# First attention of a two-block kernel: scores in plain fp32, and probabilities turned in 32x32 pieces on VectorE and moved inside SBUF

## The chip, the cores and the metric

The kernel runs on one core of one Trainium2 chip. The metric is device time in microseconds (us), the median of several runs. Engines: PE is TensorE (PEld its weight loads), DVE VectorE, ACT ScalarE, POOL GpSimd, SP SyncE. A suffix q (SPq, POOLq) is an engine's own sequencer, which issues DMAs. SBUF is the on-chip memory of 128 partitions, PSUM the banks that PE writes.

## The reference

Two layers on one sequence of 512 tokens and 1024 channels. The first has a convolution mixer and a dilated attention of 8 heads of 64 channels, and a gated feed-forward; the second has a state-space mixer and a sparse attention. The change touches the first attention:

```python
q = rms_norm(q.reshape(B, S, N_HEADS, HEAD_DIM), g_q[l]) * (HEAD_DIM ** -0.5)
k = rms_norm(k.reshape(B, S, N_HEADS, HEAD_DIM), g_k[l])
y_attn = dilated_mixture(q, k, v).reshape(B, S, D_ATTN)
# dilated_mixture: for (window, dil) in ((128, 1), (512, 4), (2048, 16)) a causal, strided
# softmax attention; the three outputs are mixed by softmax of their log-sum-exp
```

All three branches come to one causal softmax over 512 keys whose scores have log(count of branches that hold the pair) added, or a large negative number. That is how the kernel computes it: scores, plus mask1, row maximum, exp, division by the row sum, product with v.

## The kernel before

Tokens lie on the free axis: q, k and v of two heads (a pair) are tiles of 128 channels by 512 tokens. TB = 4 blocks of 128 tokens, four pairs (NPAIR). The program is written by hand, engine by engine, and each engine's order is the order of its code; semaphores tie them together.

**Weights.** SP loads a weight slot of 128x1024 into raw (L349), ACT copies its high part to wH (split_hi, L1051), DVE subtracts for the low part wL (split_lo, L1491), and PE's `project` runs 24 matmuls on it (L573 to L575). Two buffers take turns, so the load of slot n waits for the low half of slot n - 2, the high half of slot n for PE's end with slot n - 2.

**The first attention.** `mix(i, last)` runs for each pair, three times in a loop and a last time behind it. On PE a round is: projections of u, gc, gb (the convolution's three parts), a turn of v (four PE transposes of vT into PB[3], which ACT copies to vtok), the scores, the projections of the next q, k, v (`qkv`), `attend`, and `head_sums`. Scores (`split_scores`, L613 and L614): q and k are split into a high and a low part on ACT and DVE (key_high, key_low, tiles q1, k1, k1L), stacked over 128 rows, and each block of queries takes two matmuls, head 0's four blocks first. `attend`: for each head and key block PE transposes the normalised probabilities L block by block into PSUM (L550), ACT copies them to pT (p_evac), and then the products with v (L639) run over both heads; fp32 matmuls leave two records each.

**On DVE**, `score_max` adds the mask and takes the row maximum (one operation a block, L1636), negating the four maxima of a head before the next head's; then a split_lo, ssc and mixL, two of six mod_rows, and `normalise` (a reciprocal and four scalings a head, then the semaphore pn). The other mod_rows stand between the later split_lo. **On ACT** `softmax` does eight exp with a row sum (L1142). **On POOL** `mod_loads` loads six tiles of 512 KB (mraw, two buffers, L434), each when mod_rows has freed its buffer; mod_rows (L1670) multiplies them into macc, the modulation of the second layer.

The second attention has its own copy of this: `scores` (L607), plain fp32 on 64 rows with the two heads in turn, and `head_max` (L1649), which takes all eight maxima before one negation; it also uses `attend`, with t_free and tr_mm counted on by a fixed number of transposes a round. qk_norm (L1623, L1625) makes qn and kn at the start of a round on DVE, behind the last mod_rows of the round before.

## Time and profile before

| | us |
|---|---|
| median of 3 runs | 1007.5 (1007.38 to 1007.88) |
| profiled execution, its own time | 1008.97 |
| its span, first to last instruction | 1007.4 |
| PE busy | 987.2 |
| DVE busy | 680.3 |
| ACT busy | 439.3 |
| POOL busy | 155.2 |
| mean granted clock of PE | 0.994 |

The busy times are to be read against the span: PE works nearly all of it. The rows of a timeline give the start, the busy time, and in square brackets the idle time ahead of an instruction with what ended it. Records of PE overlap (a matmul's end is modelled), so its steps are read from start to start: a 128x512 matmul is recorded as 0.39 us and the next starts 0.23 us later. Granted clock 1.00 is 2.4 GHz, 0.50 is 1.2 GHz.

### The profile page before, as it was taken

The numbers are of one execution on the slowest core, as the hardware profiler recorded it, in microseconds if no ns is written. First come the engines' busy times: TensorE is split into PE (matmuls) and PEld (weight loads), VectorE is DVE, ScalarE is ACT, GpSimd is POOL, SyncE is SP. The second block draws the span as 40 slices with busy tenths as digits, with TensorE's granted clock in tenths as the row PEclk, the third lists the DMA queues.
The fourth block names the chain that finished last, engine by engine and source line by source line (L and its number), as shares of the span: only waits on it lengthen the run. The fifth ranks groups of instructions, "written<-read, shape, count | busy, mean of one in ns | idle before, by whom it ended". The sixth has DMA issues, their size and how long they took to land.

```text
span 1007.4 us, 14453 instructions
## 1 busy us (share of the span) xinstructions
PE 987.2 (98%) x4734; PEld 802.0 (80%) x4734; DVE 680.3 (68%) x1210; ACT 439.3 (44%) x725; POOL 155.2 (15%) x270
## 2 busy tenths in 40 slices
PE   6999999999999999999999999999999999999996
PEld 6887787777888888888888886888888887767886
DVE  5786786797766656645526568498978764665655
ACT  4656667543333332332311236945552334553333
POOL 3000100110000000864000000835750000000000
PEclk8999999999999999999999999999999999999998
DMA  6245534252533233244232223332233332112322
GB/s 209 85 133 160 171 99 146 66 146 83 153 117 104 86 102 103 85 146 142 90 104 88 99 75 105 98 87 68 64 105 100 87 105 63 44 62 84 104 84 84
DMA packets 145168, 104.11 MB, mean 103 GB/s; under 512 B 4636, under 2 KB 136988, under 8 KB 145132
## 3 DMA queue, kind: packets, MB, share of 16 engines
q1 hardware_dynamic: 139792, 85.96, 28.6%
q0 software_dynamic: 5104, 17.64, 5.7%
q8 instruction: 19, 0.31, 0.1%
q14 instruction: 17, 0.14, 0.0%
q10 hardware_dynamic: 236, 0.06, 0.0%
HBM read 99.45 MB, written 4.19 MB: 103 GB/s over the span
## 4 chain that ended last, share of the span: by engine, by line
PE 95%; ACT 2%; DVE 1%; issue 1%; DMA 1%; SPq 0%; DVEq 0%; ACTq 0%
PE bank L573 19%; PE bank L575 19%; PE bank L574 19%; PE bank L819 4%; PE bank L818 4%; PE bank L817 4%; PE bank L550 3%; PE bank L557 2%; PE bank L558 2%; PE bank L559 2%; PE bank L639 2%; PE bank L726 1%; PE bank L728 1%; PE bank L727 1%; PE bank L613 1%
## 5 line engine op out<-in xcount | busy, mean ns | idle before, releaser
L573 PE MATMUL bank<-hH,wH 128*128 128x512 f32 x840 | 328.6, 391 | 0.0
L575 PE MATMUL bank<-hH,wL 128*128 128x512 f32 x840 | 326.9, 389 | 0.0
L574 PE MATMUL bank<-hL,wH 128*128 128x512 f32 x840 | 326.9, 389 | 0.0
L1051 ACT ACTIVATE wH<-raw 128x1024 fp32r<-128x1024 f32 x155 | 164.2, 1060 | 270.6 <-PE bank L575 134.9
L1491 DVE TENSOR_TENSOR wL<-raw,wH 128x1024 fp32r<-128x1024 f32 x155 | 196.5, 1268 | 125.5 <-ACT wH L1051 124.6
L573 PEld LDWEIGHTS bank<-hH,wH 128*128 128x128 f32 x840 | 157.7, 188 | 36.2 <-issue 2.4
L575 PEld LDWEIGHTS bank<-hH,wL 128*128 128x128 f32 x840 | 157.7, 188 | 33.0
L574 PEld LDWEIGHTS bank<-hL,wH 128*128 128x128 f32 x840 | 157.7, 188 | 32.2
L819 PE MATMUL bank<-aH,wL 128*128 (+1 forms) x176 | 68.5, 389 | 0.0
L817 PE MATMUL bank<-aH,wH 128*128 (+1 forms) x176 | 68.5, 389 | 0.0
L818 PE MATMUL bank<-aL,wH 128*128 (+1 forms) x176 | 68.5, 389 | 0.0
L1800 DVE TENSOR_TENSOR ut<-bank,r 128x512 f32<-128x512 f32 x22 | 15.2, 691 | 49.9 <-PE bank L575 49.9
L434 POOL DMA_DIRECT2D mraw<-in_w_mod_dram x24 | 12.7, 529 | 202.4 <-DVE macc L1670 202.0
L1142 ACT ACTIVATE L<-L,nmx 128x128 f32<-128x128 f32 (+1 forms) x64 | 35.1, 550 | 11.5 <-DVE nmx L1652 10.7
L817 PEld LDWEIGHTS bank<-aH,wH 128*128 128x128 f32 x176 | 33.0, 188 | 6.9
L818 PEld LDWEIGHTS bank<-aL,wH 128*128 128x128 f32 x176 | 33.0, 188 | 6.9
L819 PEld LDWEIGHTS bank<-aH,wL 128*128 128x128 f32 x176 | 33.0, 188 | 6.7
L1670 DVE SCALAR_TENSOR_TENSOR macc<-mraw,csil,macc 128x1024 f32<-128x1024 f32 x24 | 30.2, 1281 | 9.6 <-DMA mraw<-in_w_mod_dram 9.6
L1051 ACT ACTIVATE aH<-a 128x512 f32 (+1 forms) x22 | 13.9, 632 | 45.9 <-DVE a L1804 45.9
L489 POOL COPY yaF<-yg 32x128 f32<-32x128 f32 x64 | 33.0, 515 | 2.9
L1806 DVE TENSOR_TENSOR aL<-a,aH 128x512 fp32r<-128x512 f32 (+1 forms) x22 | 17.2, 782 | 18.3 <-ACT aH L1051 18.3
L483 POOL DMA_DIRECT2D ebuf<-rotations x4 | 2.2, 563 | 154.8 <-PE bank L819 132.0
(465 smaller groups left out, 1520.0 us busy)
## 6 DMA issues: line engine op xcount, KB each, us to landing
raw<-in_w_in_dram SPq DMA_DIRECT2D x61, 512.0 KB, 3.5
mraw<-in_w_mod_dram POOLq DMA_DIRECT2D x24, 512.0 KB, 4.6
raw<-in_w_gate_dram SPq DMA_DIRECT2D x22, 512.0 KB, 3.6
raw<-in_w_up_dram SPq DMA_DIRECT2D x22, 512.0 KB, 3.5
raw<-in_w_down_dram SPq DMA_DIRECT2D x22, 512.0 KB, 3.2
raw<-in_w_out_dram SPq DMA_DIRECT2D x16, 512.0 KB, 3.5
x_tok<-in_x_dram SPq DMA_DIRECT2D x4, 512.0 KB, 7.4
rotations<-eb POOLq DMA_DIRECT2D x4, 512.0 KB, 5.1
```

The lines of the kernel that those rows point to most:

```text
L489: ins = g.tensor_copy(dst(a, b), src(a, b))
L550: ins = nc.tensor.transpose(dst[0:m, t * P:t * P + kk], src, idn[0:kk, 0:kk])
L573: mm(o, a, hH[:, k, :], start=(k == 0), stop=False)
L574: mm(o, a, hL[:, k, :], start=False, stop=False)
L575: ins = mm(o, b, hH[:, k, :], start=False, stop=(k == KD - 1))
L817: mm(PB[d][:], blk(wH[s], d), rh, start=a, stop=False, skip_group_check=True)
L818: mm(PB[d][:], blk(wH[s], d), rl, start=False, stop=False, skip_group_check=True)
L819: ins = mm(PB[d][:], blk(wL[s], d), rh, start=False, stop=z, skip_group_check=True)
L1051: return A(o, i_, ACT.Copy, scale=scale)
L1142: ins = A(l, l, ACT.Exp, bias=nmx[:, c:c + 1], accum_out=rs[:, c:c + 1])
L1491: TT(wL[s.par][:], raw[s.par][:], wH[s.par][:].bitcast(F32), SU).then_inc(lo_done, 1)
L1670: STT(o, mraw[m % 2][:], col(csil, i * 2 + m // 3), o, MU, AD).then_inc(m_used, 1)
```

## The change

Of the first attention, in all four rounds: the split of q and k and `split_scores` are gone, `scores(i, qn, kn)` and `head_max` take their place, so the heads come in turn and the maxima are negated once, at the end.

In the three rounds of the loop: DVE's transpose turns each 32x32 piece of the normalised probabilities of a query block into the tile `turned`, four instructions a head; POOL then issues four transfers inside SBUF which carry the 32 partitions of each quarter to 128 partitions of `pTd`, so that token 32j + p of a key block stands on partition 4p + j. ACT's copy of v to vT puts its tokens in the same order. `attend_turned` waits for the transfers and for the bank of the output, and has only the products with v, 8 matmuls as before, reading pTd by blocks of 32. The PE transposes of L and ACT's p_evac are gone from these rounds. On DVE the low half for v's slot now stands between head 1's scaling and its turns, mod_rows 0 and 1 move behind the turns, 2 and 3 behind the next split, 4 and 5 behind the one after. On POOL the transfers stand between mod_loads 1 and 2.

In the last round `attend` stays; v's four transposes become 16 fp32 matmuls with a strided 32-column part of vT as weights and the unit matrix as the moving operand, which undoes the new order of vT.

```diff
@@ -224,9 +225,8 @@
         wkH, wkL = at("wkH", [P, 2, P], F32R, A0 + 28704), at("wkL", [P, 2, P], F32R, A0 + 29728)
         mred, mfold = at("mred", [P, 96], F32, B0 + 4096), at("mfold", [32, 3, 96], F32, B0 + 4608)
-        q1 = [at(f"q1{e}", [P, S], F32R, B0 + 26624 + 2048 * e) for e in range(2)]
-        k1 = [at(f"k1{e}", [P, S], F32R, B0 + 30720 + 2048 * e) for e in range(2)]
-        k1L = [at(f"k1L{e}", [P, S], F32R, B0 + 34816 + 2048 * e) for e in range(2)]
+        turned = at("turned", [P, TB, 2 * NB, 32], F32, B0 + 26624)
+        pTd = at("pTd", [P, TB, 2 * NB, 32], F32, B0 + 10240)
         qx = [at("qx0", [P, S], F32R, B0 + 20480), at("qx1", [P, S], F32R, B0 + 12288)]
         kx, kxL = at("kx", [P, S], F32R, B0 + 14336), at("kxL", [P, S], F32R, B0 + 16384)
...
         def freed(eng, s):
             eng.wait_ge(gfree[s.par], s.gf + 1)
+        def places(hh, qb):
+            return slice(1 + qb, 1 + qb + 5 * qb + 1, 5) if hh == 0 else slice(5 * qb, 6 * qb + 1)
+        def place_of(hh, kb):
+            return slice(5 * kb + 1 + kb, 5 * kb + 1 + TB) if hh == 0 else slice(6 * kb, 5 * (TB - 1) + kb + 1, 5)
...
             pool.dma_start(mask1[:], consts[:, C_M1:C_END]).then_inc(mask_in, 16)
-            def mod_loads(i):
+            def turned_moves(a):
+                pool.wait_ge(turn_rdy, 2 * TB * (a + 1))
+                pool.wait_ge(turn_used, a + 1)
+                settled(pool)
+                for q in range(TB):
+                    pool.dma_start(pTd[:, q].rearrange("p b c -> p (b c)"),
+                                   turned[32 * q:32 * q + 32].rearrange("p j b c -> p j (b c)")).then_inc(turn_in, 16)
+            def mod_loads(i, between=None):
                 for m in range(6):
+                    if m == 2 and between is not None:
+                        between()
                     pool.wait_ge(m_used, i * 6 + (m + 2))
                     pool.dma_start(mraw[m % 2][:], w_mod_2[0][bass.ds(i * (2 * P) + (m // 3) * P, P),
                                                              (m % 3) * D:(m % 3 + 1) * D]).then_inc(m_full[m % 2], 16)
             with pool.Fori(0, NPAIR - 1) as i:
-                mod_loads(i)
+                mod_loads(i, lambda: turned_moves(i))
             pool.wait_ge(lo_done, N_WO + 2)
             for s in range(2):
...
@@ -613,27 +633,34 @@
                 mm(o[:, 0:n], q[:, blkc(b)], k[:, 0:n], start=True, stop=False)
                 return mm(o[:, 0:n], q[:, blkc(b)], kl[:, 0:n], start=False, stop=True)
-            def split_scores(a):
-                for hh in range(2):
-                    for b in range(TB):
-                        pe.wait_ge(sc_free, a * 8 + (4 * hh + b + 1))
-                        split_score(SB[b], b, q1[hh], k1[hh], k1L[hh]).then_inc(sc_ready, 1)
             def blkc(b):
                 return slice(b * P, (b + 1) * P)
-            def attend(a, v, vcol):
+            def attend_turned(a, v, vcol):
+                pe.wait_ge(turn_in, 16 * TB * (a + 1))
+                wait(pe, o_free, a + 1)
+                for kb in range(TB):
+                    for hh in range(2):
+                        r = slice(HD * hh, HD * hh + HD)
+                        ins = mm(OB[r, P * kb:S], v[:, kb, vcol(hh)],
+                                 pTd[:, :, place_of(hh, kb), :].rearrange("p i b c -> p b i c"),
+                                 start=(kb == 0), stop=(kb == TB - 1), skip_group_check=True)
+                        if kb == TB - 1:
+                            ins.then_inc(pv, 1)
+                pe.nop().then_inc(turn_used, 1)
+            def attend(a, n, v, vcol):
                 for hh in range(2):
                     pe.wait_ge(pn, a * 2 + (hh + 1))
                     for kb in range(TB):
-                        pe.wait_ge(t_free, a * 8 + (4 * hh + kb + 1))
+                        pe.wait_ge(t_free, n * 8 + (4 * hh + kb + 1))
                         transposes(TBANK[kb], [L[:, hh, CB[b] + P * kb:CB[b] + P * kb + P] for b in range(kb, TB)]
                                    ).then_inc(tr_mm, 1)
                 wait(pe, o_free, a + 1)
                 for kb in range(TB):
-                    pe.wait_ge(t_free, a * 8 + (kb + 9))
+                    pe.wait_ge(t_free, n * 8 + (kb + 9))
                     for hh in range(2):
                         r = slice(HD * hh, HD * hh + HD)
                         ins = mm(OB[r, P * kb:S], v[:, kb, vcol(hh)], pT[:, hh, OFF[kb]:OFF[kb + 1]],
...
                 for j in range(3):
                     project(Slot(3, j, 6, i))
                 freed(pe, Slot(2, 0, 6, i))
-                transposes(PB[3], [vT[:, blkc(b)] for b in range(TB)]).then_inc(vtr, 1)
+                if last:
+                    for b in range(TB):
+                        for j in range(TB):
+                            ins = mm(PB[3][32 * j:32 * j + 32, blkc(b)], vT[:, P * b + j:P * b + P:TB], ident,
+                                     start=True, stop=True, skip_group_check=True)
+                    ins.then_inc(vtr, 1)
+                else:
+                    transposes(PB[3], [vT[:, blkc(b)] for b in range(TB)]).then_inc(vtr, 1)
                 pe.wait_ge(ss_rd, i * 2 + 2)
                 pe.wait_ge(xt_done, KD)
-                pe.wait_ge(q_lo, i + 1)
-                split_scores(i)
+                pe.wait_ge(qn_rdy, i * 2 + 2)
+                scores(i, qn, kn)
                 if not last:
                     qkv(6, i)
...
                 pe.wait_ge(vt_done, i + 1)
                 if last:
                     mm(PB[3][:], ones[:], ssc[:], start=True, stop=True).then_inc(ssm, 1)
-                attend(i, vtok, lambda hh: slice(HD * hh, HD * hh + HD))
+                if last:
+                    attend(i, 0, vtok, lambda hh: slice(HD * hh, HD * hh + HD))
+                else:
+                    attend_turned(i, vtok, lambda hh: slice(HD * hh, HD * hh + HD))
                 if not last:
                     head_sums(i + 1, Slot(7, 0, 6, i))
...
                     between()
                 used(s[2])
                 wait(act, vtr, a)
-                copy(vT[:], PB[s[2].par][:]).then_inc(gfree[s[2].par], 1)
+                copy(vT[:].rearrange("n (b p j) -> n b p j", b=TB, j=TB),
+                     PB[s[2].par][:].rearrange("n (b j p) -> n b p j", b=TB, j=TB)).then_inc(gfree[s[2].par], 1)
             def head_rsqrt(a):
...
                 dve.wait_ge(sc_free, a * 8 + (2 * TB + 4))
                 TS(nmx[:], mx[:], -1.0, None, MU).then_inc(nm, 2)
-            def normalise(a):
+            def turn(hh, qb):
+                v.transpose(turned[:, :, places(hh, qb), :].rearrange("p j b c -> p b j c"),
+                            L[:, hh, CB[qb]:CB[qb + 1]].rearrange("p (b j c) -> p b j c", j=TB, c=32)
+                            ).then_inc(turn_rdy, 1)
+            def normalise(a, turning=None):
                 for hh in range(2):
                     dve.wait_ge(ex, a * 2 + (hh + 1))
                     mark(v.reciprocal(rinv[:, 4 * hh:4 * hh + 4], rs[:, 4 * hh:4 * hh + 4]))
@@ -1660,6 +1680,13 @@
                         l = L[:, hh, CB[b]:CB[b + 1]]
                         ins = TS(l, l, rinv[:, 4 * hh + b:4 * hh + b + 1], None, MU)
                     ins.then_inc(pn, 1)
+                    if turning is not None:
+                        if hh:
+                            turning()
+                        dve.wait_ge(pn, a * 2 + (hh + 1))
+                        dve.wait_ge(turn_used, a + 1)
+                        for b in range(TB):
+                            turn(hh, b)
             def mod_rows(i, ms):
...
                 TT(yc[:], PB[gb.par][:], cv[:], MU).then_inc(gfree[gb.par], 1)
                 masks1 = [mask1[:, S - P * (b + 1):S] for b in range(TB)]
                 if last:
-                    score_max(i, masks1, lambda: split_lo(gb.next()))
+                    head_max(i, masks1, lambda: split_lo(gb.next()))
                 else:
-                    score_max(i, masks1)
+                    head_max(i, masks1)
                     split_lo(gb.next())
                 dve.wait_ge(ych, i + 2)
                 mark(TT(ssc[:], ssc[:], sqc[:], AD))
@@ -1710,9 +1726,7 @@
                 if last:
                     need()
                     dve.nop().then_inc(cv_split, 1)
-                if not last:
-                    mod_rows(i, range(0, 2))
-                normalise(i)
+                normalise(i, None if last else lambda: split_lo(Slot(3, 3, 6, i).next()))
                 if last:
                     dve.wait_ge(astep, 1)
                     need(mean(PB[3][:], 1.0 / HALF, nt1[:]))
@@ -1720,11 +1734,11 @@
                     dve.wait_ge(rr, 1)
                     need(newton(rc[:], nt1[:], nt2[:]))
                 else:
-                    split_lo(Slot(3, 3, 6, i).next())
+                    mod_rows(i, range(0, 2))
+                    split_lo(Slot(3, 4, 6, i).next())
                     mod_rows(i, range(2, 4))
-                    split_lo(Slot(3, 4, 6, i).next())
+                    split_lo(Slot(3, 5, 6, i).next())
                     mod_rows(i, range(4, 6))
-                    split_lo(Slot(3, 5, 6, i).next())
                 dve.wait_ge(o_free, i + 2)
                 mark(TT(ssa[:], ssa[:], sqa[:], AD))
                 mark(STT(dyn(mixL, i + KH), yo[:], col(vec, i + V_GATT), dyn(mixH, i + KH).bitcast(F32), MU, SU))
```

## Rows read from the trace of the kernel before

**Rows 1.** The page: part 1 (busy us), part 3 (software queue), part 4 (chain).

```profile
PE 987.2 (98%) x4734; PEld 802.0 (80%) x4734; DVE 680.3 (68%) x1210; ACT 439.3 (44%) x725; POOL 155.2 (15%) x270
...
q0 software_dynamic: 5104, 17.64, 5.7%
...
PE 95%; ACT 2%; DVE 1%; issue 1%; DMA 1%; SPq 0%; DVEq 0%; ACTq 0%
```

**Rows 2.** Timeline, PE, first round: start us, us, line, op, out<-in, count.

```profile
57.34 0.60 PE L550 MATMUL bank<-cst,vT 128*128 128x128 f32 x4
57.69 0.30 PE L613 MATMUL bank<-k,q 128*128 128x128 f32 x1
...
60.70 0.40 PE L573 MATMUL bank<-hH,wH 128*128 128x512 f32 x1
...
77.04 1.25 PE L550 MATMUL bank<-cst,L 128*128 128x128 f32 x10
...
79.78 2.37 PE L639 MATMUL bank<-pT,vtok 128*64 128x512 f32 x16
```

**Rows 3.** Timeline, PE: scores of the second attention; 32-column products.

```profile
829.34 3.02 PE L607 MATMUL bank<-kn,qn 64*128 64x128 f32 x16
...
832.29 0.50 PE L573 MATMUL bank<-hH,wH 128*128 128x512 f32 x1
...
608.48 1.95 PE L842 MATMUL bank<-s5W,cTt 128*32 128x128 f32 x64
```

**Rows 4.** Timeline, DVE: first round, second attention; last, groups by line.

```profile
58.32 0.28 DVE L1636 CUSTOM_DVE_ANT_0 L<-bank,mask 128x128 f32<-128x128 f32 x1
...
62.24 1.23 DVE L1491 TENSOR_TENSOR wL<-raw,wH 128x1024 fp32r<-128x1024 f32 x1
...
64.64 2.48 DVE L1670 SCALAR_TENSOR_TENSOR macc<-mraw,csil,macc 128x1024 f32<-128x1024 f32 x2
67.03 0.17 DVE L1657 RECIPROCAL rinv<-rs 128x4 f32<-128x4 f32 x1
...
68.45 0.16 DVE L1657 RECIPROCAL rinv<-rs 128x4 f32<-128x4 f32 x1
...
91.65 1.23 DVE L1491 TENSOR_TENSOR wL<-raw,wH 128x1024 fp32r<-128x1024 f32 x1
...
829.96 0.29 DVE L1649 CUSTOM_DVE_ANT_0 L<-bank,score 128x128 f32<-128x128 f32 x1 [0.95 <-PE bank L607]
...
833.74 0.17 DVE L1652 TENSOR_SCALAR nmx<-mx 128x8 f32<-128x8 f32 x1
...
L1852 DVE STREAM_TRANSPOSE mtr<-macc 128x1024 f32<-128x1024 f32 x3 | 3.7, 1237 | 0.0
```

**Rows 5.** Timeline, ACT, first round.

```profile
60.31 0.40 ACT L1142 ACTIVATE L<-L,nmx 128x128 f32<-128x128 f32 x1
...
64.60 0.19 ACT L1142 ACTIVATION_READ_ACCUMULATOR L<-L,nmx 128x1 f32 x1
66.36 0.60 ACT L1051 ACTIVATE qraw<-bank 128x512 f32<-128x512 f32 x1 [1.57 <-PE bank L575]
```

**Rows 6.** Timeline, POOL, first round; the tile mraw: issue to landing.

```profile
72.89 0.53 POOL L434 DMA_DIRECT2D mraw<-in_w_mod_dram  x1 [4.58 <-DVE macc L1670]
...
DMA to landing us min/median/max: 3.6/4.6/7.1
```

**Rows 7.** Busy time by stretch; the last three columns are clock, DMA share, GB/s.

```profile
72.00:80.00 8.00, 7.79 (x45) 6.38 (x46) 4.24 (x5) 5.29 (x12) 1.05 (x2) 1.00 0.81 247
9.70:11.70 2.00, 0.00 (x0) 0.00 (x0) 1.39 (x5) 1.26 (x5) 0.00 (x0) 1.00 1.14 348
...
13.00:18.90 5.90, 5.89 (x28) 5.89 (x29) 4.66 (x13) 4.23 (x7) 1.64 (x3) 0.50 0.33 91
```

**Rows 8.** Waits of PE, 835 to 925 us: who for whom, us, times, longest.

```profile
PE bank L557 <- ACT thg L1395: 1.6, 1, 1.6
```

**Rows 9.** Timeline, PE, last round: the products with v.

```profile
196.52 2.37 PE L639 MATMUL bank<-pT,vtok 128*64 128x512 f32 x16
```

More of the change, by code:

```diff
@@ L77 @@
 OFF = [0, 512, 896, 1152, 1280]
+NB = 10
 V_GMIX, V_CONV, V_GCONV, V_GATT, V_GFFN, V_C, V_NG, V_BMOD, V_BGLU, V_DSK, V_FG, V_GQ, V_GK = \
@@ L270, in program @@
         ss_mm, ss_rd, rs_rdy, qn_rdy = (sem(n) for n in ("ss_mm", "ss_rd", "rs_rdy", "qn_rdy"))
-        q_hi, q_lo, qx_hi, kx_hi = (sem(n) for n in ("q_hi", "q_lo", "qx_hi", "kx_hi"))
+        qx_hi, kx_hi, turn_rdy, turn_in, turn_used = (
+            sem(n) for n in ("qx_hi", "kx_hi", "turn_rdy", "turn_in", "turn_used"))
         vtr, vt_done, ych = sem("vtr"), sem("vt_done"), sem("ych")
@@ L642, in attend @@
                             ins.then_inc(pv, 1)
-            for s in (ix_ready, xf_tr):
+            for s in (ix_ready, xf_tr, turn_used):
                 pe.nop().then_inc(s, 1)
@@ L1400, in att @@
                     copy(qn[:], PB[0][:], HD ** -0.5).then_inc(gfree[0], 1)
-                p_evac(i + NPAIR)
+                p_evac(i + 1)
                 freed(act, s)
```

40 lines of the change are left out of this document (4 added, 36 removed).

## The prediction, made before the changed kernel ran

> **What bounds the kernel now.** I read the page first: busy times, then the chain that ended last. TensorE (PE) is busy 987.2 of 1007.4 us and holds 95% of the chain [rows 1]. So the time changes by what is added to or taken from PE's own queue, or by a new gap in it; work on the other engines counts only through such a gap. Then I read the timeline of PE over the first round of the loop (rounds are 42.23 us apart, three of them, and a last round outside the loop). The reader is to see four marks [rows 2]: the scores start at 57.69, the q, k, v projections at 60.70, the 20 turns of the probabilities by PE at 77.04, and the products with v at 79.78. So the projections give 16.34 us of cover for the softmax, and the turns cost PE 79.78 - 77.04 = 2.74 us, the copies from PSUM among them. That 2.74 us in three rounds, 8.2 us, is all that the change can win on PE there. The same timeline for VectorE (DVE) and ScalarE (ACT) tells when the probabilities are ready [rows 4, 5].
>
> **Scores.** Before, 16 matmuls of split operands take 60.70 - 57.69 = 3.01 us [rows 2]. The new form, fp32 with 64 rows and the heads in turn, stands in the second attention: 829.34 to 832.29, 2.95 us for 16 records, with DVE's first maximum at the same distance (0.62 us) behind the start [rows 3, 4]. Gain 0.06 us a round, 0.2 us in three; PE reaches the end of the projections at 76.98 instead of 77.04. Bounds: 0 and -0.4 us a round (the second attention's two halves apart would run without waits). The splitting of q and k that goes away on ACT and DVE lay beside projections, and PE waited for none of it, so it is worth nothing directly.
>
> **When the probabilities are turned.** One chain decides, so I walk it, on the clock of round one.
> 1. All eight maxima now come before one negation. The chain before has the first maximum at 58.32 [rows 4]; the second attention needs 833.74 - 829.96 = 3.78 us to the negation [rows 4]. So the maxima are ready at 62.27.
> 2. ACT's eight exponentials took 60.31 to 64.78 [rows 5], 4.47 us, back to back. They now start at 62.3, so head 0 is done at 64.5, head 1 at 66.8. q, evacuated at 66.36 before [rows 5], waits 0.4 us for that.
> 3. DVE meanwhile does the low half of a weight slot, ssc and mixL: 62.24 to 64.64 [rows 4], as before. The first two rows of the modulation (mod_rows, 2.4 us) are moved behind, so normalising head 0 starts at 64.6 instead of 67.03. One head's reciprocal and four scalings take 68.45 - 67.03 = 1.42 us [rows 4]: 66.05.
> 4. Four turns of head 0: the only DVE turn in the trace is 128x1024 in 1237 ns [rows 4]. 1280 columns in four instructions are, at that rate per column plus about 0.1 us each, 1.75 us. Bounds 1.55 (rate alone) and 3.0 (if the strided blocks halve the rate). I take 1.75: it is the same instruction on the same type. 67.95.
> 5. Head 1's scalings, 1.42 us, then the low half for v's slot, 1.14 us, are done at 70.5. PE wants that slot at 60.64 + 10.9 = 71.5, so 1.0 us is left as cover; turns slower by over that would stop PE here too.
> 6. Four turns of head 1, 1.75 us: 72.3.
> 7. POOL issues four transfers, 0.53 us each [rows 6], from 72.4 to about 74.7.
>
> **The transfers**, which no row of before shows (none goes from SBUF to SBUF), carry 4 x 327,680 B = 1.31 MB. The shortest load of mraw lands 3.6 us after its issue [rows 6]; 524 KB at the software queue's own rate (17.64 MB in 5.7% of 16 engines' 1007.4 us is 307 GB/s [rows 1, 6]) are 1.7 us of it, so the start costs about 1.85 us and the first bytes move at 74.25. Then bounds: at 348 GB/s, the most that I find over 2 us [rows 7], 3.8 us, landing at 78.0; at half of 307 GB/s 8.5 us, landing at 82.8. I take the mixed traffic of just this place, 247 GB/s over 72 to 80 us [rows 7], because SP's load of the next slot is issued at about 76 (behind the low half that frees it) and another is just ending at 74. 1.31 MB and 0.2 MB of theirs at 247 GB/s are 6.1 us: landing at 80.35.
>
> The products start at 80.4 where they started at 79.78 [rows 2]: +0.65 us a round, +2.0 us in three. Bounds: 78.1 (-1.7 a round) and 82.9 (+3.1). So 2.74 us of turns become 3.4 us of waiting. The products themselves keep their 16 records and columns; I price the strided reading of 32-column blocks at nothing (runs of 128 B; the second bound of it, half rate, would be +2.3 us a round, and nothing in the trace asks for it).
>
> A rule of the Trainium skill, SBUF — State Buffer, "Door 1: The DMA port swizzle", speaks against the change: 32 neighbouring partitions reach only 8 of 16 ports of 27.2 GB/s. Each transfer reads 32 partitions. By it 1.31 MB take 6.0 us, about what I take from the row; by the whole fabric of the same section, 436 GB/s, 3.0 us and the sum would be some 9 us lower. No row here shows either, the rows are all of transfers over 128 partitions.
>
> **The clock.** PE now stands still for 3.4 us; in the middle of the span its longest wait is 1.6 us [rows 8]. The trace shows what that can do: PE idle from 9.7 to 11.7, busy for 0.3 us up to 13.0, and then the granted clock is 0.50, that is 1.2 GHz, through 5.9 us of work [rows 7]. One such fall costs half of 5.9, 3.0 us. Bounds: none of the three waits, or all three (0 and +8.9 us). I take one: these waits are as long as that idle time, but end in dense work.
>
> **Behind the wait.** turned_moves stands in POOL's queue ahead of the third load of mraw, and DVE's mod_rows wait for those loads. Counted on from the landing L of the moves: row 2's load lies behind them in the queue and lands at L + 1.75, row 2 ends at L + 3.1 (1.28 us a row), row 3 at L + 4.7; the loads for rows 4 and 5 are issued as these end and take 4.3 to 4.6 us [rows 6], so row 5 ends at about L + 10.3. Then ssa and mixL (1.35), the q and k norms (1.35) and the low half of gb's slot (1.2): L + 14.2. Before, that low half ran from 91.65 [rows 4]. PE wants it at L + 0.1 + 2.3 + 1.0 + 10.9 = L + 14.3. So it is just in time, priced at nothing, with PE's own products and projections as its cover; without it each us of delay costs 1 us in each of three rounds.
>
> **The last round** keeps the turns on PE. The v turn becomes 16 fp32 matmuls of 32 columns of weights, 32 records. The same form stands in the trace: 64 records in 1.95 us, 1.7 us start to start [rows 3], so 0.86 us against 0.35 (57.34 to 57.69): +0.5 us. If the strided weights cost as much as the first score records (107 ns each) it is +3.1. But the softmax chain is later too: maxima from 185.1 (0.2 us later than before, since the v turn delays the scores), 1.15 us for four small ones, 1.14 for a split, 2.18 for four large ones, negation at 189.8; exponentials to 194.25; head 1 normalised at 195.75. The turns of head 1 then end at 197.1 and the products start at 197.3 where they started at 196.52 [rows 9]. The 0.5 us lies under this wait. +0.8 us.
>
> **Sum.** -0.2 + 2.0 + 3.0 + 0.8 = +5.6 us. The profiled execution took 1008.97 us around a span of 1007.4; the median of the three runs is 1007.5, 1.5 us less, of which the change alters nothing. So 1014.6 for a profiled one, and 1007.5 + 5.6 = 1013.1 as the median.
>
> **Rivals.**
> *The transfers are quick.* They run at 348 GB/s in spite of the load beside them and land at about 78.0 to 79.0. Then the products start 0.7 to 1.7 us earlier a round, the wait is 1 to 2 us, shorter than the idle time before the clock's fall, and there is none. -0.2 - 3 x 1.2 + 0.8 = -3.0: 1004.5. This is the case on the other side, and it decides at one point: landing before 79.5. For it: the queue between 66 and 71 us is empty now, and a move inside SBUF needs no HBM. Against it: the load of the next slot starts in the middle, and four issues alone take until 74.7. Chance 0.32.
> *The transfers are late, the clock stays.* -0.2 + 2.0 + 0.8 = +2.6: 1010.1. For it: no gap of a like length among dense matmuls is in the trace. Chance 0.22, a part of it within the band of no change.
> *Another wait takes over.* The turns run at half rate: 1.5 us later per head, so v's slot stops PE for 0.5 us and the moves land 2.5 to 3 us later; or gb's slot comes late by 1 to 2 us. With two falls of the clock: 0.6 + 3 x 2.5 + 6 = +14: 1021.5. For it: there is no turn into strided blocks in the trace. Chance 0.10.
> *The forecast*, late by 0.3 to 1 us a round and with one or two falls: 1010.5 to 1017. Chance 0.36.
>
> **How the numbers follow.** The likeliest is 1013.1. For 8 in 10 the range takes in the quick transfers down to 1003 and the bound of the slow ones up to 1020; what is left out is mostly the third rival. A measurement of this kernel can tell 0.2%, 2 us, from no change. Faster by more: most of the quick case, 0.30. Within: its slow end and the best of the second rival, 0.14. Slower: 0.56.
>
> **What would show it.** In the profile after: the first v product of each round starting at 80.4 (right) or before 79.5 (the quick case), with its idle time released by the moves; POOL's four issues beginning at 72.4, and DVE's turns of 512 columns near 0.65 us; the granted clock in the 10 us behind each wait at 1.00 or below; the low half of gb's slot against the start of gb's projection; PE's records of the v turn in the last round near 27 ns apart. The forecast is wrong if the landing is off by more than 1 us, for each us counts three times and decides about the clock with it.

## The result and the profile after

The changed kernel takes 1026.9 us (median of 4 runs, 1025.4 to 1027.7) where the kernel before takes 1007.4 beside it: a ratio of 1.0192, 95% interval 1.0174 to 1.0209. It is slower, as forecast, but by 19.5 us and not 5.6, and the time lies outside the range. The profiled execution has a span of 1026.1 us against 1007.4. Of all executions reported below one, of e12, took 2795.9 us; e12's ratio is without it.

The page of the changed kernel, part 1 (busy us) and part 4 (the chain that ended last):

```profile
PE 987.7 (96%) x4702; PEld 793.6 (77%) x4702; DVE 672.5 (66%) x1206; ACT 415.7 (41%) x677; POOL 162.5 (16%) x282
...
PE 86%; DVE 4%; DMA 4%; issue 2%; ACT 2%; POOL 0%; DVEq 0%; SPq 0%; POOLq 0%; ACTq 0%
```

PE is as busy as before (987.7 against 987.2 us), though 60 turns left it, and its share of the chain fell from 95% [rows 1] to 86%. New gaps in PE, then, and slower work in it. The waits of PE (who for whom, us in total, times, longest) name the gap:

```profile
PE bank L646 <- DMA pTd<-turned: 18.0, 3, 6.1
...
PE bank L570 <- ACT pT L1088: 1.0, 2, 0.9
PE bank L593 <- DVE wL L1519: 0.9, 1, 0.9
```

The first round in time, PE: turn of v, scores, start and end of the projections, products with v, head sums, next projections (the answer to [rows 2]); then VectorE (to [rows 4]), then POOL (to [rows 6]):

```profile
55.66 0.60 PE L570 MATMUL bank<-cst,vT 128*128 128x128 f32 x4
56.18 3.11 PE L627 MATMUL bank<-kn,qn 64*128 64x128 f32 x16
59.23 0.50 PE L593 MATMUL bank<-hH,wH 128*128 128x512 f32 x1
59.56 0.40 PE L594 MATMUL bank<-hL,wH 128*128 128x512 f32 x1
...
75.45 0.39 PE L595 MATMUL bank<-hH,wL 128*128 128x512 f32 x1
81.98 3.77 PE L646 MATMUL bank<-pTd,vtok 128*64 128x512 f32 x16 [6.14 <-DMA pTd<-turned]
...
86.70 0.50 PE L593 MATMUL bank<-hH,wH 128*128 128x512 f32 x1
```

```profile
60.60 0.17 DVE L1666 TENSOR_SCALAR nmx<-mx 128x8 f32<-128x8 f32 x1
...
63.34 1.27 DVE L1681 TENSOR_SCALAR L<-L,rinv 128x128 f32<-128x128 f32 x4
64.65 1.69 DVE L1670 STREAM_TRANSPOSE turned<-L 128x128 f32<-128x128 f32 x4
...
68.76 1.68 DVE L1670 STREAM_TRANSPOSE turned<-L 128x128 f32<-128x128 f32 x4
70.37 2.44 DVE L1697 SCALAR_TENSOR_TENSOR macc<-mraw,csil,macc 128x1024 f32<-128x1024 f32 x2
84.56 1.28 DVE L1697 SCALAR_TENSOR_TENSOR macc<-mraw,csil,macc 128x1024 f32<-128x1024 f32 x1 [10.12 <-DMA mraw<-in_w_mod_dram]
...
90.28 1.28 DVE L1697 SCALAR_TENSOR_TENSOR macc<-mraw,csil,macc 128x1024 f32<-128x1024 f32 x1 [1.75 <-DMA mraw<-in_w_mod_dram]
93.74 1.28 DVE L1697 SCALAR_TENSOR_TENSOR macc<-mraw,csil,macc 128x1024 f32<-128x1024 f32 x1 [2.18 <-DMA mraw<-in_w_mod_dram]
...
97.53 1.22 DVE L1519 TENSOR_TENSOR wL<-raw,wH 128x1024 fp32r<-128x1024 f32 x1
```

```profile
71.14 2.18 POOL L446 DMA_DIRECT2D pTd<-turned  x4 [54.26 <-DVE turned L1670]
73.25 1.25 POOL L454 DMA_DIRECT2D mraw<-in_w_mod_dram  x2
```

Two things are to be seen: everything up to the issue of the moves went as forecast, and the moves then took 10.84 us from the first issue (71.14) to the first product (81.98). This execution reached its first scores 1.5 us earlier than the profiled one of before; the profiled executions below start anywhere between 55.26 (e2) and 58.16 (e10), so that offset belongs to the execution and not to the change, and distances are read from the scores or the issue on.

Busy time by stretch over the wait (stretch and length, busy us of PE, PEld, DVE, ACT, POOL, granted clock, DMA share, GB/s), against [rows 7]:

```profile
76.00:78.00 2.00, 0.00 (x0) 0.00 (x0) 0.00 (x0) 1.42 (x2) 0.00 (x0) 1.00 0.87 222
78.00:80.00 2.00, 0.00 (x0) 0.00 (x0) 0.00 (x0) 0.00 (x0) 0.00 (x0) 0.50 0.92 289
80.00:82.00 2.00, 0.02 (x2) 0.02 (x2) 0.00 (x0) 0.00 (x0) 0.00 (x0) 0.50 0.99 312
82.00:84.00 2.00, 2.00 (x6) 0.74 (x8) 0.00 (x0) 0.00 (x0) 0.00 (x0) 0.50 0.66 234
84.00:86.00 2.00, 2.00 (x16) 0.86 (x16) 1.28 (x1) 0.18 (x1) 0.00 (x0) 0.79 0.30 98
```

The clock fell to 0.50 (1.2 GHz) while PE stood idle, 2.2 us into the gap in this round and 4.6 and 3.8 us into it in the next two, and it was still there for the products: 3.77 us for what took 2.3 before, 4.54 us in the second and in the third round (products at 130.69 and 178.98). It was back at 1.00 only 2.9, 5.4 and 4.8 us behind the first product, so in the last two rounds the head sums were slow as well. Rounds are 48.7 to 48.9 us apart where they were 42.23.

### The profile page after: what moved, and what is told of

It is laid out like the page before. It is cut to its first block, busy times and chain, and to the rows that moved or that the text cites. A ratio compares the mean times of both kernels' runs of the same rounds, so it can differ in the third digit from the quotient of the medians.

```text
span 1026.1 us, 14336 instructions
## 1 busy us (share of the span) xinstructions
PE 987.7 (96%) x4702; PEld 793.6 (77%) x4702; DVE 672.5 (66%) x1206; ACT 415.7 (41%) x677; POOL 162.5 (16%) x282
## 4 chain that ended last, share of the span: by engine, by line
PE 86%; DVE 4%; DMA 4%; issue 2%; ACT 2%; POOL 0%; DVEq 0%; SPq 0%; POOLq 0%; ACTq 0%
PE bank L593 17%; PE bank L595 17%; PE bank L594 17%; PE bank L856 4%; PE bank L855 4%; PE bank L854 4%; PE bank L577 2%; PE bank L570 2%; PE bank L578 2%; PE bank L579 2%; DMA pTd<-turned 2%; DMA mraw<-in_w_mod_dram 2%; PE bank L627 2%; PE bank L763 1%; PE bank L765 1%
## 5 line engine op out<-in xcount | busy, mean ns | idle before, releaser
L646 PE MATMUL bank<-pTd,vtok 128*64 128x512 f32 (+3 forms) x48 | 12.8, 708 | 18.0 <-DMA pTd<-turned 18.0
L1820 DVE TENSOR_TENSOR aL<-a,aH 128x512 fp32r<-128x512 f32 (+1 forms) x22 | 16.9, 770 | 18.3 <-ACT aH L1088 18.3
```

## The experiments

The theory formed from this trace, **P**: the moves are slow by themselves, because each reads only 32 partitions of SBUF. Its rivals: **C**, the loads of mraw and the weights beside them slow them down; **F**, each move or each run costs a fixed time. And for the second part of the loss, **the clock**: PE at half clock behind the wait costs about 2 us a round. In the table, "issue to products" is from POOL's first issue of a move to the first product, in the three rounds. In e5, e6 and e8 ScalarE's queue issues its first move 0.5 to 0.6 us before POOL's.

| kernel | median us | ratio to before, 95% | issue to products | PE waits for moves, us (longest) |
|---|---|---|---|---|
| after | 1026.9 | 1.0174 to 1.0209 | 10.8, 10.9, 10.5 | 18.0 (6.1) |
| e1 loads held back | 1034.4 | 1.0252 to 1.0291 | 11.6, 11.1, 10.9 | 19.3 (6.9) |
| e2 filled wait | 1027.5 | 1.0176 to 1.0210 | 10.2, 11.2, 10.9 | 1.6 (1.0) |
| e3 scores only | 1008.9 | 1.0006 to 1.0025 | | |
| e4 straight moves | 1009.1 | 1.0007 to 1.0026 | 6.6, 5.7, 5.7 | 3.8 (1.9) |
| e5 two queues by half | 1019.1 | 1.0108 to 1.0142 | 7.7, 7.9, 8.4 | 9.8 (3.6) |
| e6 two queues mixed | 1024.9 | 1.0162 to 1.0196 | 10.0, 9.8, 10.1 | 15.8 (5.4) |
| e7 small rows | 1025.8 | 1.0167 to 1.0201 | 10.5, 10.8, 10.8 | 17.9 (6.1) |
| e8 two queues, rotated | 1018.2 | 1.0090 to 1.0124 | 8.6, 8.0, 10.2 | 12.6 (5.4) |
| e9 filled wait, small rows | 1020.0 | 1.0112 to 1.0143 | 10.8, 10.9, 10.7 | 1.8 (0.7) |
| e10 half the bytes | 1012.7 | 1.0033 to 1.0063 | 5.2, 5.3, 5.1 | 1.4 (0.6) |
| e11 one head each | 1010.9 | 1.0022 to 1.0050 | | none |
| e12 one head, paired | 1008.4 | 1.0000 to 1.0019 | | none |

### e1: the loads behind the moves held back

```
                 for q in range(TB):
                     pool.dma_start(pTd[:, q]..., turned[32 * q:32 * q + 32]...).then_inc(turn_in, 16)
+                pool.wait_ge(turn_in, 16 * TB * (a + 1))
```

> The changed kernel, but POOL waits for the four moves to land before it issues the next two mraw loads. Theory C (the moves are slow because the two 512 KB mraw loads issued right behind them share the DMA engines): the moves land 2 to 3 us earlier, PE's wait at the products falls from 6.1 to 3 to 4 us a round, 1017 to 1020 us. Theory P (the moves are slow by themselves, each reading only 32 partitions): the landing moves by less than 0.7 us, the wait stays at 5.5 to 6 us, and since the loads come some 8 us later, the low half for gb's slot stops PE for 2 us or more a round: 1028 to 1036 us.

1034.4 us. Without the two loads of mraw beside them the moves are no quicker: 11.6, 11.1 and 10.9 us. C is refuted for these loads. What rises is the wait behind: the loads come later, VectorE's rows with them, and PE waits 5.8 us in three places for the low half of a slot (0.9 us in the changed kernel). The rows behind the wait thus had no cover left to give.

### e2: PE kept at work during the wait

```
+                pe.wait_ge(sc_free, a * 8 + 12)
+                for _ in range(24):
+                    mm(PB[4][:], hL[:, 0, 0:P], hH[:, 0, :], start=True, stop=True)
                 pe.wait_ge(turn_in, 16 * TB * (a + 1))
```

> The changed kernel, but PE runs 24 matmuls of 128x512 on idle data (5.5 us, their result is thrown away) while it waits for the moves. Theory clock (the products with v take 4.5 us in place of 2.3 because the granted clock fell during the wait): products at 2.3 us, clock 1.00 throughout, 2.5 us a round less, 1019 to 1020 us. Rival (the products are slow because they read pTd in strided blocks of 32): the products stay near 4.5 us, 1026 to 1028 us.

The timeline of PE, round one, and PE's two longest kinds of wait in the loop:

```profile
74.75 5.60 PE L643 MATMUL bank<-hH,hL 128*128 128x512 f32 x24
80.42 2.38 PE L649 MATMUL bank<-pTd,vtok 128*64 128x512 f32 x16
```

```profile
PE bank L593 <- DVE wL L1522: 6.6, 3, 2.6
PE bank L649 <- DMA pTd<-turned: 1.6, 2, 1.0
```

The products are back at 2.38 us: it was the idle time that brought the clock down, and not the reading of pTd in blocks of 32 that made them slow. But the time stays, 1027.5. What the products gave back, PE waits for the low half of gb's slot (6.6 us for 0.9). PE gets it 17.2, 16.1 and 16.9 us after the first product, and 16.8 us in the changed kernel's first round (98.81 against 81.98), however quick the products are. And the clock is not up throughout in this kernel: it falls behind the gb wait of the first and of the third round (2.61 and 2.38 us), here in the first (columns as above):

```profile
98.60:101.90 3.30, 3.30 (x9) 2.56 (x8) 2.72 (x4) 0.00 (x0) 0.00 (x0) 0.50 0.68 201
```

The rounds with such a fall take 50.0 and 51.0 us (the latter with 0.5 us of the last round's v turn in it); the second round, with a wait of 1.63 us and no fall, takes 48.3. One of the four executions has a mean clock of 0.997 for the others' 0.994, and it took 1024.8 us for their 1027.4 to 1030.1.

### e3: the new scores alone

The kernel before, with the scores and maxima of the change in all four rounds and the turns left to PE:

```
-                pe.wait_ge(q_lo, i + 1)
-                split_scores(i)
+                pe.wait_ge(qn_rdy, i * 2 + 2)
+                scores(i, qn, kn)
...
-                    score_max(i, masks1)
+                    head_max(i, masks1)
```

> The kernel before with the new scores and head_max alone, the turns staying on PE in all four rounds. My sum: 0.06 us a round less on PE and +0.8 us in the last round where the softmax is later: 1007.5 to 1008.5 us. Rival (the new scores themselves carry a part of the 19 us, through the later start of the exponentials): over 1010 us.

+1.5 us (10 runs, interval +0.6 to +2.5). PE's scores start at 55.50 and end at 58.54, 3.04 us, no quicker than the split ones; rounds are 42.55 us for 42.23. In the last round head 1's turns wait:

```profile
192.57 1.25 PE L550 MATMUL bank<-cst,L 128*128 128x128 f32 x10
194.68 1.31 PE L550 MATMUL bank<-cst,L 128*128 128x128 f32 x10 [0.85 <-ACT pT L1051]
```

The row names ScalarE, whose four copies of head 0 end at the same moment. But the first turn of head 1 needs only the first of them; the other thing that it needs, head 1 normalised, is done by VectorE at 194.61:

```profile
193.34 1.27 DVE L1655 TENSOR_SCALAR L<-L,rinv 128x128 f32<-128x128 f32 x4
```

### e4: the same bytes over 128 partitions

Each move carries the same 327,680 bytes in rows of 2560, but from 128 partitions to the same 128. The blocks then stand in other places than the products expect; what is left out is the exchange between partitions, the rest of the work is the same.

```
-    pool.dma_start(pTd[:, q]..., turned[32 * q:32 * q + 32].rearrange("p j b c -> p j (b c)"))
+    pool.dma_start(pTd[:, q]..., turned[:, q].rearrange("p b c -> p (b c)"))
```

> The changed kernel, but each of the four moves reads one quarter of the columns of all 128 partitions and writes them to the same partitions of pTd: same bytes, same run of 2560 B, same count, only the source is spread over 128 partitions; the keys end up misplaced, so the attention's values are wrong, the work is the same. Theory P (32 source partitions halve the rate): the moves land 3 to 4 us earlier, wait 2 to 3 us, the clock falls less: 1011 to 1018 us. Theory C (contention with loads): landing within 0.5 us of the changed kernel's, 1025 to 1028 us.

```profile
77.52 2.38 PE L646 MATMUL bank<-pTd,vtok 128*64 128x512 f32 x16 [1.87 <-DMA pTd<-turned]
...
119.74 2.37 PE L646 MATMUL bank<-pTd,vtok 128*64 128x512 f32 x16 [0.93 <-DMA pTd<-turned]
```

1009.1 us: 17.8 of the 19.5 us are gone with one edit, in what a move reads. Issue to products is 5.7 to 6.6 us for 10.5 to 10.9, the waits are 0.9 to 1.9 us and the clock stays up. The trace records the packets of the moves (the pieces in which the DMA engines carry them), 256 a round of 5120 B in either kernel: one takes 0.24 us on average here and 0.40 to 0.41 in the changed kernel, so it is the single packet that is slow, and there are no more of them. The edit changes a second thing with the first, that each row stays on its own partition; no run tests that alone. e5 and e6 below keep the exchange and still find that the source partitions matter, which is why I put it down to them.

### e5 and e6: two queues

Two of the four moves are issued by ScalarE's queue. In e5 POOL has those that read partitions 0 to 63 (q of 0 and 1), ScalarE those that read 64 to 127; in e6 each has one of either half (0, 2 and 1, 3). The diff of e5 (PE waits for both queues in it):

```
-                for q in range(TB):
+                for q in (0, 1):
...
+                        act.wait_ge(turn_rdy, 2 * TB * a)
+                        act.wait_ge(turn_used, a)
+                        for q in (2, 3):
+                            act.dma_start(pTd[:, q]..., turned[32 * q:32 * q + 32]...).then_inc(turn_in2, 16)
```

> The changed kernel, but only the moves that read partitions 0 to 31 and 32 to 63 are issued by POOL; those that read 64 to 95 and 96 to 127 are issued by ACT at the same time, on its own queue. Theory P, with the halves 0 to 63 and 64 to 127 of SBUF on different ports: both halves move at once, the moves land 3 to 4 us earlier, the clock falls less often, and the wait for gb's slot takes a part: 1011 to 1018 us. Rival (each move is slow for another reason, as the engines' work on short source ranges, whichever half): landing within 1 us of the changed kernel's, 1023 to 1028 us.

> As the two-queue kernel, but POOL has the moves that read partitions 0 to 31 and 64 to 95, ACT those that read 32 to 63 and 96 to 127, so that both queues read the lower half first and the upper half then. Theory P with halves: hardly better than one queue, landing at most 1 us earlier, 1023 to 1027 us. Rival (two queues are quicker whatever they read): the same as the other two-queue kernel, 1011 to 1018 us.

By half, issue to products is 7.7 to 8.4 us (1019.1 us); mixed, it is 9.8 to 10.1 (1024.9). Counted from ScalarE's issue, which comes first, it is 8.3 to 8.9 and 10.4 to 10.7, so mixed queues gain next to nothing over the one queue's 10.5 to 10.9. Both kernels have two queues and issue at the same times; the gain of some 2 us comes only when each queue keeps to its own half of the partitions. In e6 both queues issue a move of the lower half first and then one of the upper; this is no clean opposite of e5, though: if each queue works in order, the packets' records (half of ScalarE's bytes moved 3.9 us behind its issue, half of POOL's 6.5) have unlike halves side by side for some 2.6 us of it. The waits of e5 are still 3.0 to 3.6 us, the clock fell in or just behind each of them (at 79.28 in the first round, 0.3 us behind the first product), and the products take 4.0 to 4.5 us.

### e7: small loads and rows

In the three rounds the loads of mraw and VectorE's rows on them are cut to 64 of 1024 columns (the modulation of the other columns is left out).

```
-    pool.dma_start(mraw[m % 2][:], ...(m % 3) * D:(m % 3 + 1) * D])
+    w = D if isinstance(i, int) else 64
+    pool.dma_start(mraw[m % 2][:, 0:w], ...(m % 3) * D:(m % 3) * D + w])
```

> The changed kernel with the modulation's loads and rows of the three rounds cut from 1024 to 64 columns (that work is left out, so the second layer's modulation is wrong). Theory P: the moves land as in the changed kernel to within 1 us, PE waits 5 to 6 us and the clock falls in each round; only the wait for gb's slot goes, 1024 to 1027 us. Theory C: without 3 MB of loads a round the moves land 2 to 3 us earlier, 1015 to 1019 us.

1025.8 us, issue to products 10.5 to 10.8 us. With 16 times fewer bytes of mraw beside them the moves still take as long; that settles C for mraw. The loads of the weights, the other half of C, bring 0.08 to 0.13 MB while the moves run in the changed kernel and 0.36 to 0.39 MB here, by the packets' records, and the moves take no longer for it. PE's waits for a slot are gone, and all that brings is 1.0 us, which lies within the two intervals.

### e9: filled wait and small rows

The two edits of e2 and e7 together, in order to see what the clock costs when nothing stands behind it.

> The changed kernel with both covers of the clock's price gone: the 24 further products of e2 stand in the wait, and in the rounds the mraw loads and the row work on them are cut to 64 columns as in e7 (values of macc are wrong for it). Theory (the clock costs about 2.2 us a round, and in e2 the slot of gb's low half took that place): products begin as in the changed kernel, about 10.8 us after the first move's issue, run at 2.3 to 2.5 us for 16, granted clock 0.99 or more, no wait for gb or wL over 1 us, and the time falls by 5 to 7 us below the changed kernel, to 1020 to 1022. Rival (the products at half clock cost nothing, since VectorE's row or something else behind them is due as late anyway): the products are as quick, the time stays within 2 us of e7, 1024 to 1028, and another wait has grown to 2 us a round.

```profile
81.37 2.38 PE L650 MATMUL bank<-pTd,vtok 128*64 128x512 f32 x16 [0.65 <-DMA pTd<-turned]
```

1020.0 us. Against e7, which differs only in the filler, 5.9 us are gone, 2.0 a round: that is the price of the clock's three falls. It fits the trace of e7, where the clock is at 0.50 for 12.6 us of work behind the waits, half of which is 6.3. The price was real, and in e2 the gb slot's lateness of the same size, with two falls of its own, had taken its place. The two costs lie side by side, so taking away one alone gives nothing.

### e10: half the bytes

Each move carries 10 of the 20 blocks, in rows of 1280 bytes; the other half of pTd stays zero, so half of the blocks are left out.

```
-    pool.dma_start(pTd[:, q]..., turned[32 * q:32 * q + 32].rearrange("p j b c -> p j (b c)"))
+    pool.dma_start(pTd[:, q, 0:NB]..., turned[32 * q:32 * q + 32, :, 0:NB].rearrange("p j b c -> p j (b c)"))
```

> The changed kernel, but each of the four moves carries 10 of the 20 blocks of a partition: half the bytes, the same partitions and the same number of runs, each 1280 bytes for 2560 (the other half of pTd stays zero, so the attention output is wrong). Theory P (the move is limited by a rate, about 150 GB/s from 32 source partitions, behind a start of about 1.85 us): the products begin about 4.3 us earlier, 6.2 to 6.8 us after the first move's issue; PE's wait for them falls from 6.1 to about 1.8 us, the clock stays, 1009 to 1013. Rival F (a fixed cost for each of the moves, or for each run, limits them): the products begin less than 1.5 us earlier, over 9.3 us after the issue, PE waits 4.6 us or more, 1021 or more.

Issue to products is 5.2 us: 5.6 less for half the bytes and as many moves and runs. F is refuted: with as many moves and rows it is the size that decides. (The moves' packets are 5120 B here too, and half as many, so this kernel doesn't tell bytes from packets; e4, with all 256, does.) But the size is off from P's simple form (1.85 us and then 150 GB/s gives 6.2): the halves differ, the second 0.66 MB costs 5.6 us, 118 GB/s, the first 0.66 MB 3.4 us behind the start, 195 GB/s. So the rate isn't one number. The packets tell where it sinks: in the first round of the changed kernel three quarters of the bytes have been moved 7.2 us behind the issue and the last quarter takes 3.2 us more; here the last quarter takes 0.9. Why there is such a tail is open. The waits tell of the next limit:

```profile
PE bank L594 <- DVE wL L1520: 6.2, 3, 2.8
PE bank L647 <- DMA pTd<-turned: 1.4, 3, 0.6
```

With the moves in time, the slot of gb is late by 2.1 us a round on average, and in the second round, behind a wait of 2.05 us, the clock falls to 0.50 for 3.4 us. That is why this kernel stands at 1012.7 and not below the kernel before.

### e8: two queues, and VectorE's order changed

e5, and besides: VectorE norms q and k and splits gb's slot before its rows 4 and 5 in each round, and the last round is scored head by head as before.

```
-                    mod_rows(i, range(4, 6))
...
+                    qk_norm(i + 1)
+                    split_lo(Slot(9, 0, 6, i).next())
+                    mod_rows(i, range(4, 6))
```

> A try at a version that beats both: the moves on two queues by halves; on DVE the q and k norms and the low half of gb's slot moved ahead of the last two modulation rows; the last round's scores head by head with two negations as before the change. If the moves land 3 to 4 us earlier and the wait for gb's slot goes: 2 us of wait a round in place of 2.74 us of turns, clock 1.00: 1004 to 1009 us. If the halves don't move at once: 1020 to 1026 us.

1018.2 us for e5's 1019.1, within each other's intervals. The profiled execution is the slowest of its four (1021.2 us): the moves took 8.6, 8.0 and 10.2 us and the waits for them rose from 9.8 to 12.6 us. No wait for a slot is left, but e5 has none either, and the low half of gb's slot starts at 92.54, where e5 has it at 92.58; here it waits 3.98 us for ScalarE's high half. So the new order of VectorE's rows is neither shown to help nor to harm.

### e11 and e12: one head by each way

Head 0 is turned by VectorE and moved (13 block places, 0.85 MB, rows of 1664 bytes), head 1 by PE and ScalarE as before. That issues the moves one head earlier, and PE's turns of head 1 cover their end. (The last round is scored head by head, as before.)

```
+                pe.wait_ge(pn, a * 2 + 2)
+                for kb in range(TB):
+                    transposes(TBANK[kb], [L[:, 1, ...] for b in range(kb, TB)]).then_inc(tr_mm, 1)
                 pe.wait_ge(turn_in, 16 * TB * (a + 1))
```

> A middle way: head 0 alone is turned on VectorE in 32x32 pieces and moved (13 blocks a partition, 0.85 MB for 1.31 MB, rows of 1664 bytes), head 1 is turned by TensorE and evacuated by ScalarE as in the kernel before; the last round is scored head by head as before. By theory P the moves, issued at about 66.5, land 0.85 MB / 150 GB/s + 1.85 = 7.5 us later at about 74, ahead of the end of the projections at about 75.3: no wait of PE on a transfer over 1 us, clock 0.98 or more, each round shorter by head 0's PE turns (about 1.3 us) less 0.3 for the scores: 1004 to 1006.5, faster than both. Rival (the moves meet the weights' and rows' traffic, or VectorE's turns push its row and the low half behind the rest): a wait of 1 us or more in each round and 1008 or more.

The trace of e11, second round, PE:

```profile
118.50 1.25 PE L571 MATMUL bank<-cst,L 128*128 128x128 f32 x10
119.68 1.93 PE L656 MATMUL bank<-pTd,vtok 128*64 128x512 f32 x5
121.24 0.64 PE L656 MATMUL bank<-pT,vtok 128*64 128x512 f32 x1
...
122.15 1.46 PE L656 MATMUL bank<-pT,vtok 128*64 128x384 f32 x6
123.54 0.65 PE L726 MATMUL bank<-sqq,ones 64*64 64x512 f32 x2
```

No wait for a move is left, and the mean clock is 0.997. By the packets' records the last bytes have been moved 8.7, 7.3 and 7.3 us behind the issue, where the theory had the landing at 7.5; the projections and PE's turns cover them. But the time, 1010.9 us, is the rival's, and by a mechanism that neither of them named. The products now take 3.86 us (119.68 to 123.54) where the kernel before has 2.3. I had put them one head after the other, to let ScalarE finish head 1. Products of the two heads write different halves of the bank's partitions, and in turn they run at once; one after the other they don't. e12 pairs them again, puts ScalarE's evacuations of head 1 ahead of v's, and scores the last round with the heads in turn:

```
-                for hh in range(2):
-                    for kb in range(TB):
+                for kb in range(TB):
+                    pe.wait_ge(t_free, a * 4 + (kb + 5))
+                    for hh in range(2):
```

> As e11 (head 0 by VectorE and transfers, head 1 by TensorE), with the products of the two heads in turn within each block again, as in the kernels before and after, ScalarE's four evacuations of head 1 ahead of v's, and the last round scored with the heads in turn. Theory: in e11 the products of one head, then of the other took 3.85 us from the first of them to the head sums (119.68 to 123.54) where the kernel before takes 2.3 (122.01 to 124.31), and that is what ate head 0's saved transposes: paired, each of three rounds gets 1.0 to 1.5 us shorter (42.54 down to 41.0 to 41.5), the last some 0.6, the rows otherwise as in e11: 1005.5 to 1007.5, at or just under the kernel before. Rival (the products wait for head 1's last evacuation by as much as the pairing saves): rounds of 42.2 or more, PE waits on pT of 1 us a round, 1009.5 or more.

```profile
121.09 0.64 PE L655 MATMUL bank<-pTd,vtok 128*64 128x512 f32 x1
121.09 0.64 PE L655 MATMUL bank<-pT,vtok 128*64 128x512 f32 x1
...
123.39 0.65 PE L725 MATMUL bank<-sqq,ones 64*64 64x512 f32 x2
```

The pair starts at the same 121.09, and the 16 take 2.3 us. The second round is 41.1 us (scores at 100.30 and 141.41), 1.1 under the kernel before. Still the kernel is at 1008.4, interval 1.0000 to 1.0019: the first and the third round keep a wait of 1.0 and of 0.9 us for gb's slot, the turn of v for the last round in small pieces and the last round's chain cost what the rounds gave. What each of these three took is not tested by itself. None of the versions beats the kernel before.

## Why the prediction was wrong, point by point

- **Bound, cover, order of the chain**: right. PE's queue sets the time, and the loss is a gap in it.
- **When the probabilities are turned**: right within 0.4 us at each step. From the first scores: negation at 4.42 us (forecast 4.58), turns of one head 1.69 us (1.75, and not the bound of 3.0), moves issued at 71.14 - 56.18 = 14.96 (72.4 - 57.69 = 14.7). Four issues take 2.18 us (72.4 to 74.7, 2.3).
- **The transfers: the step that failed.** The forecast had 80.35 - 72.4 = 7.95 us from issue to landing; it was 10.84. The start of 1.85 us left 6.1 us at 247 GB/s; in fact, behind the same start, 9.0 us went into 1.31 MB, 146 GB/s. (The start is the forecast's own; by the packets' records the first bytes move 1.1 us behind the issue and the last 10.5 us, which makes 140 GB/s.) I had named about that as the slow bound (half of 307 GB/s, landing 10.4 us after the issue) and set it aside for a rate of loads that use 128 partitions. e4 shows what the row of 247 GB/s was good for: over 128 partitions the same bytes took 5.7 to 6.6 us from issue to products, next to the other bound (5.6, at 348 GB/s). e1 and e7 show that mraw's loads played no part; the weights' load, from which I reasoned, brought 0.1 MB meanwhile, and some 0.4 MB of it in e7 made the moves no slower. The rule of the Trainium skill in SBUF — State Buffer, "Door 1: The DMA port swizzle", pointed at the right cause, and e4 and e5 against e6 agree with it in kind: the partitions read decide, and the two halves have separate ways out. In size it fell short: an estimate from its 8 ports of 27.2 GB/s makes 6.0 us of 1.31 MB, where the runs show about 9. Taking the rule's number as support for the 6.1 us of the sum was a mistake of its own: two estimates that agreed by chance.
- **Three rounds**: this step was priced at +2.0 us (0.65 a round). From the end of the projections to the first product, start to start, it is 6.3, 6.3 and 5.9 us, 18.5 in all (the idle time of 18.0 counts from a modelled end), so 18.5 - 3 x 2.74 = +10.3 us.
- **The clock**: one fall at 3.0 us was forecast. There were three, as in the upper bound, but each is worth 2.0 us (e9 against e7: 5.9 in all), since only the products and the head sums lie in it. The products went from 2.3 to 3.8 to 4.5 us. The term was mis-sized by 2.9 us, and it followed from the wait's length: 3.4 us forecast, 6.1 measured. The rival in which the clock stays is refuted even for a wait of 3 to 3.6 us (e5). Transfers and clock at their upper bounds, +9.3 and +8.9, with the other terms, would have made 1026.3; the range stopped at 1020, though late transfers are just what brings the clock down.
- **Behind the wait**: gb's low half was to be done at L + 14.2 us against a need at L + 14.3. It was done at 98.7 with L = 81.98, L + 16.7. The failed piece is the loads for rows 4 and 5: the second of them took 5.7 us (issued at 88.03, its row at 93.74), forecast 4.3 to 4.6, and row 2 had ended 0.8 us late. The rows end at L + 13.0 and not L + 10.3, with a gap of 1.75 and of 2.18 us ahead of them. The slow clock hid 1.5 to 2.2 us of that, so only 0.9 us of waits shows in the changed kernel; e2 and e10 bring it to light (6.6 and 6.2 us). The sentence on what it costs without cover held; that the cover would be the falling clock itself it didn't say.
- **Scores**: -0.2 us forecast, +1.5 measured with the last round's share in it (e3). A round took 0.32 us more, and the rows show where: the step from v's turn to the scores is 0.52 us for 0.35 (55.66 to 56.18; 57.34 to 57.69 before), the scores are 3.05 us and not 2.95, for 3.01, and the step from the first matmul of the projection to the second is 0.33 us for 0.23. The forecast priced the scores alone, and not their edges.
- **The last round**: +0.8 forecast. From v's turn to the products it is 215.41 - 201.41 = 14.00 us against 12.50 before, +1.5. The pieces of v's turn took 1.05 us up to the scores (0.86 forecast; the records stand 27 ns apart on average, as named, and the step to the scores is the longer one of the other rounds). The failed piece is the sentence that this lies under the softmax chain: the maxima were set at 185.1, 1.1 us behind v's turn, but they wait for the scores and started 1.7 us behind it (203.09 against 201.41; e3, without the pieces, has 1.15). From there the chain went as forecast, negation 4.6 us later (4.7) and head 1 normalised 10.8 us later (10.65). The wait of 0.9 us ahead of head 1's turns is the end of this chain, as in e3: VectorE's last scaling ends at 213.92, the turns start at 213.98.

The terms as measured, 10.3 + 5.9 + 0.9 + 1.0 (three rounds of e3's 0.32) + 1.5, are 19.6 us for the 19.5. They come from different kernels and executions, so the agreement says no more than that nothing large is missing.

## What to carry to other kernels

Before a transfer inside SBUF goes on the path, count the partitions that each piece reads, not the bytes alone: from issue to use the same 1.31 MB took 5.7 to 6.6 us out of 128 partitions and 10.5 to 10.9 us in pieces of 32. When a cost has a bound that nothing but traffic speaks against, ask which of its ends the shape of the transfer is like, and not which has the better-known rate. And where two costs lie side by side behind one wait (here a fallen clock and a late weight slot), take both away at once before judging either.

## What the hardware showed that I had not expected

- Moves from 32 partitions ran at some 150 GB/s for 1.31 MB, less than half of the 348 GB/s of [rows 7], and neither mraw's loads nor the weights' beside them mattered (e1, e7). The packets of 5120 B took 0.40 us for the 0.24 of moves from 128 partitions (e4). Half the bytes took well under half the time (3.4 us for 9.0 behind the start).
- Two queues helped only when one read partitions 0 to 63 and the other 64 to 127: 7.7 to 8.4 us from POOL's issue to the products, for 9.8 to 10.1 (e5, e6).
- TensorE's granted clock fell from 1.00 to 0.50 while the engine stood still, 2.2 to 4.6 us into the gap, and was still at 0.50 for 2.9 to 5.4 us of work behind it. It fell too in or just behind waits of 3.0 to 3.6 us (e5), 2.6 and 2.4 us (e2) and 2.05 us (e10), and not at those of 0.9 to 1.9 us (e4) nor at one of 2.8 us (e10). So waits between 2 and 3 us went either way.
- fp32 products into the two halves of a bank's partitions run at once when they alternate: 2.3 us for 16, and 3.86 us when one half follows the other.
